# One matmul per token block gathers several jobs' tokens; expert outputs are gated and added straight onto the scaled residual; the last LayerNorm's weights move to VectorE

## The reference

```
h = _layer_norm_f32(x) * (1 + sc2) + sh2
logits = h @ w_router + b_router
top_v, top_i = lax.top_k(logits, 2);  w = softmax(top_v)
f = sum over e of combine[:, e:e+1] * (silu(h @ wg[e]) * (h @ wu[e])) @ wd[e]
x = layer_norm(ALPHA * x + gt2 * f) * ln2_g + ln2_b      # ALPHA = 4 ** 0.25
```

## Time and profile before

| | us |
|---|---|
| median of 3 runs | 2384.35 |
| lowest, highest run | 2383.2, 2392.06 |
| the profiled execution, its own time | 2378.61 |
| its span, first to last instruction | 2376.8 |
| TensorE busy | 2107.1 (89%) |
| VectorE busy | 954.2 (40%) |
| ScalarE busy | 735.3 (31%) |
| GpSimd busy | 639.2 (27%) |
| HBM read | 495.88 MB, 209 GB/s over the span |
| mean granted TensorE clock | 0.94 |

### The profile page before, as it was taken

One profiled execution on the slowest core, in us unless ns is written; L12 is line 12 of the kernel. 1 busy time (PEld: TensorE's weight loads), 2 busy tenths in 40 slices (PEclk: granted clock), 3 DMA queues, 4 the chain that ended last, 5 costly groups with the idle time before them and its releaser, 6 DMA issues.

```text
span 2376.8 us, 33465 instructions
## 1 busy us (share of the span) xinstructions
PE 2107.1 (89%) x13205; PEld 1447.8 (61%) x13205; DVE 954.2 (40%) x1437; ACT 735.3 (31%) x1025; POOL 639.2 (27%) x356
## 2 busy tenths in 40 slices
PE   6988889994999999688788589999999999998884
PEld 3444467773877778455477465666565666666563
DVE  2344531355222355534424643333434333445445
ACT  2135532224122233114423132323332223334441
POOL 0012311253122122302324212333222333323332
PEclk8999999995999999799899689999999999999996
DMA  7211024430354423111076058999967999979991
GB/s 267 92 40 36 19 89 160 168 115 21 114 183 144 133 98 100 36 47 51 26 241 230 23 231 338 406 399 418 386 261 305 395 405 421 384 315 411 420 421 55
DMA packets 151425, 499.15 MB, mean 210 GB/s; under 512 B 8268, under 2 KB 71884, under 8 KB 108132
## 3 DMA queue, kind: packets, MB, share of 16 engines
q1 hardware_dynamic: 151268, 496.96, 54.9%
HBM read 495.88 MB, written 1.05 MB: 209 GB/s over the span
## 4 chain that ended last, share of the span: by engine, by line
PE 71%; DVE 9%; issue 8%; POOL 5%; DMA 3%; ACT 2%; SPq 0%; POOLq 0%; DVEq 0%; ACTq 0%
PE psum L805 69%; POOL w_lo L2470 3%; POOL reg_p L2438 1%; PE psum L1035 1%; DMA ring<-in_w_mod 1%; DVE stat L2036 1%; DVE x_res L1919 1%; DVE reg_q L2029 1%; DMA ring<-in_w_in 1%; DVE reg_r L1918 1%; ACT w_hi L1511 1%; DVE stat L1869 1%; DVE stat L1870 0%; DMA e_ring<-in_experts 0%; DVE w_lo L1879 0%
## 5 line engine op out<-in xcount | busy, mean ns | idle before, releaser
L2470 POOL TENSOR_TENSOR w_lo<-e_ring,w_hi 128x512 fp32r<-128x512 f32 x92 | 224.1, 2437 | 519.6 <-PE psum L805 343.6
L2403 POOL TENSOR_TENSOR w_lo<-ring,w_hi 128x512 fp32r<-128x512 f32 (+1 forms) x74 | 172.7, 2334 | 546.2 <-ACT w_hi L1511 546.1
L805 PE MATMUL psum<-e_ring,reg_q 128*32 128x128 f32 (+3 forms) x4272 | 304.0, 333 | 9.0 <-issue 4.6
L1879 DVE TENSOR_TENSOR w_lo<-ring,w_hi 128x1536 fp32r<-128x1536 f32 (+1 forms) x74 | 128.6, 1741 | 369.1 <-ACT w_hi L1511 369.1
L1511 ACT ACTIVATE w_hi<-ring 128x2048 fp32r<-128x2048 f32 (+1 forms) x74 | 133.0, 1798 | 394.3 <-PE psum L805 106.1
L805 PEld LDWEIGHTS psum<-e_ring,reg_q 128*32 128x32 f32 (+1 forms) x4272 | 182.2, 120 | 114.6 <-issue 63.5
L1879 DVE TENSOR_TENSOR w_lo<-e_ring,w_hi 128x1536 fp32r<-128x1536 f32 x92 | 168.7, 1838 | 180.4 <-PE psum L805 154.3
L1781 ACT ACTIVATE w_hi<-e_ring 128x2048 fp32r<-128x2048 f32 x92 | 175.9, 1912 | 180.9 <-DMA e_ring<-in_experts 173.4
L805 PE MATMUL psum<-h_hi,w_hi 128*128 128x512 f32 x352 | 140.4, 399 | 5.5 <-issue 5.5
L805 PE MATMUL psum<-reg_q 96*128 96x512 f32 (+4 forms) x300 | 127.6, 552 | 19.1 <-ACT reg_v L1644 10.1
L805 PE MATMUL psum<-w_hi,xg_hi 128*128 128x512 f32 x336 | 135.0, 402 | 6.7 <-ACT w_hi L1781 6.5
(11 more groups left out here) (291 smaller groups left out, 3837.5 us busy)
## 6 DMA issues: line engine op xcount, KB each, us to landing
e_ring<-in_experts SPq DMA_DIRECT2D x240, 1024.0 KB, 9.7
e_more<-in_experts SPq DMA_DIRECT2D x96, 1024.0 KB, 9.7
ring<-in_w_mod SPq DMA_DIRECT2D x48, 1024.0 KB, 7.8
ring<-in_w_in SPq DMA_DIRECT2D x22, 1024.0 KB, 5.3
ring<-in_w_ff_gate SPq DMA_DIRECT2D x11, 1024.0 KB, 5.3
ring<-in_w_ff_up SPq DMA_DIRECT2D x11, 1024.0 KB, 5.5
ring<-in_w_ff_down SPq DMA_DIRECT2D x10, 1024.0 KB, 5.0
ring<-in_w_ao SPq DMA_DIRECT2D x8, 1024.0 KB, 5.3
```

What stands on the lines that cost most here:

```text
L805: ins = pe.matmul(o, lhs, rhs, start=start, stop=stop, **kw)
L1879: return dve.tensor_tensor(dst, src, hi.bitcast(F32), ALU.subtract)
L2403: pool.tensor_tensor(w_lo[:, n % SLOTS, a:size], ring[:, n % SLOTS, a:size], w_hi[:, q % HIS, a:size].bitcast(F32), ALU.subtract).then_inc ...
L2470: pool.tensor_tensor(lo_slot[slot][:, LO_DVE:SLOT], e_slot[slot][:, LO_DVE:SLOT], w_hi[:, (n_split + t) % HIS, LO_DVE:SLOT].bitcast(F32), ...
```

## The change

1. The 0/1 matrices of the heavy part and its second part lie side by side (`sel_heavy`), as do those of the two light jobs (`sel_light`), so one matmul with a moving side of 192 columns (heavy, two-job rounds) or 96 columns (light) does what two did. The outputs take banks 0 to 3 (heavy, two-job) and banks 3 and 7 (light, two-job). The light step at t=2 goes. The heavy gather of a two-job round moves from behind chunk 39 to between low(39) and high(40), since bank 3 is busy before, and waits for the last transposed block of the second part.
2. ScalarE and VectorE each modulate half of the second part (it was ScalarE alone).
3. The residual `x_res` is multiplied by ALPHA once, ahead of the rounds, by ScalarE, and is the accumulator; `f_acc` goes. Outputs are multiplied by the gate before they are scattered: the heavy output in place in PSUM, `y2` as it is copied (now by VectorE), the light ones behind their last sum with a copy of the gate laid out like them (`gate_l`).
4. At the end, `y_hi` and `y_lo` are made in halves, each tile is normalised as soon as its own weighs are done, and VectorE does weight and bias in two operations with two tensor inputs each; GpSimd has no part. TensorE uses other banks there and waits less for VectorE.
5. Semaphores are shared (`ln_in`, `route_in`), and three small matmuls that signal `hi_used` stand ahead of the first gather.

```diff
-    if two:
-        put(2, ("gather", "q"))
...
-    put(JOB_CHUNKS - 3, ("next",))
+    if two:
+        amid[JOB_CHUNKS - 2].append(("next",))
+    else:
+        put(JOB_CHUNKS - 3, ("next",))
...
+        sel_heavy, sel_light = (part(4 * P).rearrange("p (t n) -> p t n", t=2) for _ in range(2))
+        sel_tok, sel_tok2 = sel_heavy[:, :, 0:P], sel_heavy[:, :, P:2 * P]
+        sel_tok_l = {"h": sel_light[:, :, 0:P], "q": sel_light[:, :, P:2 * P]}
...
+        def heavy_at(two, k, c0, n):
+            per, wide = (2, HEAVY) if two else (4, P)
+            at = k % per * wide + c0
+            return psum[:, k // per, at:at + n]
...
             def gather(two):
+                for k in range(KD):
+                    for t in range(2):
+                        mm(heavy_at(two, k, 0, HEAVY if two else P), xn[:, t, k * P:(k + 1) * P],
+                           sel_heavy[:, t, 0:HEAVY if two else P], start=(t == 0), stop=(t == 1),
+                           sig=xg_mm if k == KD - 1 and t == 1 else None)
...
                     elif op == "next":
                         pe.wait_ge(sel_ready, g + 2)
+                        if two:
+                            pe.wait_ge(a2t_ok, j7 + NFC)
                         gather(two)
...
+            act.activation(x_res[:, 2:4, :], x_res[:, 2:4, :], ACT.Copy, scale=ALPHA).then_inc(x_scaled, 1)
...
-            def outputs_hi(base):
-                act.wait_ge(w_used, base + n_split)
-                act.activation(y_hi[:, :], psum[:, 4:6, :].rearrange("p b n -> p (b n)"), ACT.Copy).then_inc(yhi_ok, 1)
+            def outputs_hi(i):
+                for dh in range(2):
+                    act.wait_ge(y_gated, 2 * i + (dh + 1))
+                    act.activation(y_hi[:, dh * 512:(dh + 1) * 512], psum[:, 4 + dh, :], ACT.Copy).then_inc(yhi_ok, 1)
...
+            def outputs_lo(base, i):
+                dve.wait_ge(w_used, base + n_split)
+                for dh in range(2):
+                    dve.tensor_tensor(psum[:, 4 + dh, :], psum[:, 4 + dh, :], gate2[:, 1, dh * 512:(dh + 1) * 512],
+                                      ALU.mult).then_inc(y_gated, 1)
+                for dh in range(2):
+                    dve.wait_ge(yhi_ok, 2 * i + (dh + 1))
+                    cols = slice(dh * 512, (dh + 1) * 512)
+                    low(y_lo[:, cols], psum[:, 4 + dh, :], y_hi[:, cols]).then_inc(y_dve, 1)
...
+                dve.tensor_tensor(y2, psum[:, 6, :], gate_l["h"], ALU.mult).then_inc(y2_ok, 1)
...
+                        if b == NFC - 1:
+                            ins.then_inc(l_sum_ok[c], 1)
+                            dve.wait_ge(l_sum_ok[c], g + 1)
+                            ins = dve.tensor_tensor(y_l[c], y_l[c], gate_l[c], ALU.mult)
...
-                    residual(2 + t, dh, f_acc[:, t, dh * 512:(dh + 1) * 512], gate2)
-                normalise(stats_before[4] + t, x_res[:, 2 + t, :], z_sb[:, t, :], z_scaled)
+                dve.scalar_tensor_tensor(out=z_sb[:, t, :], in0=src, scalar=ln_mv[:, k % 4, 0:1], in1=ln_last[0],
+                                         op0=ALU.subtract, op1=ALU.mult).then_inc(z_scaled, 1)
...
+                dve.scalar_tensor_tensor(out=src, in0=z_sb[:, t, :], scalar=ln_rstd[:, k % 4:k % 4 + 1],
+                                         in1=ln_last[1], op0=ALU.mult, op1=ALU.add).then_inc(x_new, 1)
...
-            for t in range(2):
-                weights_of(4, 2 + t, t)
```

More of the change, by code:

```diff
@@ L497, in build @@
         at[0] = 8192
-        f_acc = part(2 * D).rearrange("p (t n) -> p t n", t=2)
+        gate_l = {"h": part(512), "q": part(256)}
         route_c = part(R_END)
@@ L583, in build @@
         x_in = [sem(f"x_in{t}") for t in range(TT)]
-        ln_in = [sem(f"ln_in{i}") for i in range(4)]
-        route_in = sem("route_in")
+        ln_in = sem("ln_in")
+        route_in = bmod_in
         out_done = sem("out_done")
@@ L2259, in weigh, with pair_body @@
                                          in1=acc, op0=ALU.mult, op1=ALU.add).then_inc(done, 1)
-            def outputs_lo(i):
-                dve.wait_ge(yhi_ok, i + 1)
-                low(y_lo[:, :], psum[:, 4:6, :].rearrange("p b n -> p (b n)"), y_hi[:, :]).then_inc(y_dve, 1)
-            def pair_body(two, g):
+            def outputs_lo(base, i):
[7 more added lines that the diff above has]
+                    low(y_lo[:, cols], psum[:, 4 + dh, :], y_hi[:, cols]).then_inc(y_dve, 1)
+            def pair_body(two, g, i=None):
                 base, _ = in_body(dve, two, g, twos)
```

177 lines of the change are left out of this document (97 added, 80 removed).

## The result

| | before | changed |
|---|---|---|
| median of 4 runs, us | 2383.77 | 2348.23 |
| lowest, highest run | 2378.55, 2392.06 | 2343.02, 2352.4 |
| span of the profiled execution | 2376.8 | 2340.9 |

The ratio is 0.9847, interval 0.9812 to 0.9881. A second measurement of the same pair gave 2345.91 against 2378.19 us (ratio 0.9854, 0.9827 to 0.9881).

What follows compares the result with a forecast made beforehand. TensorE was taken to bound the two-job rounds, transfers the one-job round, a chain of engines the end. Terms -7.3 -1.7 -0.5 +1.0 +0.5 -13.3 = -21.3 us gave a median of 2363.0 us, range 2354.5 to 2371.5.

Steps and rivals of the forecast that it cites:

- the first gather: Gather ahead of the rounds: merged into 32 records of 192 columns, 9.6 to 11.2 us; -0.5 us.
- the clock's fall behind the narrow gather: Round two, 16 records behind the narrow light gather: 1.5 us may go too, left for the lower bound, not summed.
- the starts of the rounds: New VectorE work at round starts: nothing before round two, +1.0 us before the one-job round (bounds 0 and +2.5).
- Light gathers: Two-job rounds: one 96-column gather costs 3.7 us and the second gather goes; -7.3 us over both rounds.
- Next gather: Next round's gather in two-job rounds: 7.31 us becomes 5.6, its new place gives some back; -0.85 us a round.
- The end: One-job round's end: y_l's earlier scaling +0.5 us, shorter chain without GpSimd -13.3 us (bounds -15 and -10).
- transfers as the pace: Rival, two-job rounds: transfers set the pace, the gathers' 9 us are given back, time 2372; chance 0.14.
- a merge without gain: Rival, merged gathers: 96- or 192-column records cost in full proportion to columns, little saved, time 2372; chance 0.02.
- the low clock for whole slots: Rival, round starts: TensorE falls to the low clock, 6 us more per slot, time 2399; chance 0.04.

## Why the prediction was wrong

The sum was 21.3 us; the first two profiles differ by 35.9. Three terms of the sum failed: the first gather (a low clock carried through all of it), the clock's fall behind the narrow gather (left at nothing), and the starts of the rounds (+1.0 and nothing, where both got shorter). About half of the miss is chance of this pair. Steps in its order, with the difference of the first two profiles behind the forecast:

1. **Light gathers: right.** -7.3 forecast, -7.26 measured; 96 columns cost 114 ns a record. The 1.5 us behind the narrow gather were left to the lower bound with the words "the gather alone does not bring it": that step failed. A fall that does not come each time still has a price. It came back in both further profiles of the old loops and with the gathers apart, and not once behind 96 columns: about -1.5 us in round two, and none in round one of this pair. The Trainium skill (TensorE: Matmul & The Clock Gate, HAM oscillation) lays such falls to gaps of the engine. The rows disagree here: TensorE was recorded busy 7.00 of 7 us ahead of the 0.57.
2. **Next gather: right in kind, small in size.** -0.85 a round forecast, -1.16 measured in round one. I took 5.6 us for the gather; it took 5.07, so the merge saved 2.2 us (the kernel with the gather apart says 2.0), and its new place gave back 1.0 where I had 0.85.
3. **First gather: undersized.** -0.5 forecast; -2.4 in a typical pair (21.61 or 21.79 to 19.1 to 19.4), -4.9 in the first. The other 2.3 are the chance of the first profile. I had 9.6 to 11.2 us for the gather, 200 ns a record carried over as if the low clock lasted through it whatever its length; it took 7.5 to 7.9 us in the seven typical profiles and 7.0 in the first. The clock rose from 0.50 to 1.00 inside it (3.1 us into it in the first profile):

```profile
1370.00:1373.00 3.00, 3.00 (x11) 3.00 (x11) 0.49 (x1) 0.00 (x0) 0.00 (x0) 0.50 1.03 429
1373.00:1377.00 4.00, 3.85 (x24) 3.55 (x22) 0.04 (x1) 0.12 (x1) 0.00 (x0) 1.00 1.01 426
```

4. **Start of a round: wrong twice.** Into round two I wrote "nothing". It was -1.0 to -2.0: the pause by itself was 4.55, 4.30 and 4.15 us with the old loops and 2.6 to 3.3 in nine profiles with the new ones and no early matmuls, and the 0.30 us wait for the last low split went. The early matmuls show that pauses in this stretch hang on what stands ahead of the loop: 34 matmuls gave a second pause at the same record in both of their kernels, 26 another one in both of theirs, seven none in one. Whether their count, their time or the place of the code does it was not separated. Why the new loops pause less stays open: that it has the same reason is argued, not shown. Into the one-job round I had +1.0; the stretch up to its gather was 0.3 us shorter, and the low products of chunk 0 started 3.67 us behind the gather's start in place of 3.49, so 0.2 us of the 1.0:

```profile
2095.90 0.68 DVE L2320 TENSOR_TENSOR reg_q<-psum,reg_q 128x512 f32<-128x512 f32 x1
2096.49 1.75 DVE L1902 TENSOR_TENSOR w_lo<-e_ring,w_hi 128x1536 fp32r<-128x1536 f32 x1
```

It started 3.71 us behind the first high products in place of 2.39, 1.3 us later where I had put 2.0, and the light gather covers the rest. The one-job round's own length (208.2 to 214.7 us in the profiles with the gather in its place) is set by transfers and swings by more than this step.
5. **The end: right in its chain, a little small.** -12.8 with y_l's scaling, -14.5 between the first two profiles. The chain itself came out 0.8 us shorter than reckoned (19.2 for 20.0). The other 0.9 us is the last low products, at the low clock in the first profile of before and at the full one in the second, as in the changed kernel (1.19):

```profile
2338.26 2.07 PE L805 MATMUL psum<-w_lo_more,at_hi 128*128 128x512 f32 x4 [2.34 <-DVE w_lo_more L1879]
2340.17 1.20 PE L805 MATMUL psum<-w_lo_more,at_hi 128*128 128x512 f32 x4 [2.31 <-DVE w_lo_more L1879]
```

They were slow in 2 of 3 profiles with the old order of work and in 2 of 14 with the new one. So neither order always brings it, and that the new one brings it less often is not shown.
6. **Outside the sum:** 2.4 us of the 35.9 lie ahead of the first gather, in a part whose end differs by 3.8 and 3.9 us between two profiles of one kernel. They are chance as far as these runs tell. So is the 1.6 us of the one-job round.

The difference, then: -2.4 (chance) -4.9 -3.6 -1.2 -1.3 -3.7 -2.6 -0.3 -1.6 -14.5, by stretches (rounded). Of the 14.6 us beyond the forecast, some 7.2 are chance of the first pair: 2.4 ahead of the first gather, 2.3 at it, 1.6 in the one-job round, 0.9 in the last low products. The terms that the repeats bear out are the other 7.4 or so: 2.1 at the first gather, 1.5 of clock behind the narrow gather of round two, 0.5 in the next gathers, 2.6 at the starts of the second and third round, 0.8 in the chain of the end. The second pair, without the stretch ahead of the first gather, gives 29.2 for 21.3, a miss of 7.9. With the terms that repeat, then, the gain is about 29 us, which would have left the time just inside the forecast range; the medians gained 35.5 and 32.3, and no run says where the rest of them lies. It is within the noise: the first interval (0.9812 to 0.9881) is 28 to 45 us.

I had bounded each step by what one row showed. Of the rivals, transfers as the pace and a merge without gain are refuted by the two kernels with gathers apart; the low clock for whole slots did not occur in the profiles of the changed kernel.

## What to carry to other kernels

Count a gather like this one, fp32 and with 128x128 weights, by its records and not its columns up to 128 columns (109 to 117 ns a record at the full clock for 32, 64, 96 and 128, 158 for 192), and merge neighbours into one wide moving operand. Where the granted clock falls near a narrow operation, price the fall with it. Cut two traces at the same landmarks before trusting a median, and profile each kernel twice before calling a difference its own: stretches bound by TensorE mostly repeat within 0.1 us, so half a microsecond shows where whole runs spread over 10 us. And when code is added ahead of a hardware loop, look at the loop's way back before judging the edit.

## What the hardware showed that was not expected

- TensorE pauses by itself where round one's loop goes back to round two (4.15 to 4.55 us with the old loops, 2.6 to 3.4 with the new ones), and 34 small matmuls ahead of the loop add a second pause of 4.06 or 4.40 us two records in; 26 add one of 0.88 or 1.62 us at another place; seven add none.
- In the two-job rounds the clock fell behind 32 records of 32 columns, with TensorE recorded busy, 4 times in 6, and never in 26 cases behind 96 columns. In the one-job round it was low behind such records in 5 of 17 profiles.
- Beside GpSimd's operations (2.67 and 2.72 us there, 2.34 by themselves) VectorE's operation with two SBUF operands took 2.71 us in place of 0.69, and the one with a PSUM operand stayed at 0.77 us beside them, against 0.75 alone. The Trainium skill (SBUF — State Buffer, the section on who interferes with whom) names just this condition, two SBUF inputs against a GpSimd operation that reads SBUF; the rows agree.
